# Convolution opening prepared in the projection's last tiles, and the mixer's first steps prepared in the chunk pass

## What is computed

```python
def implicit_filters(L, w1, b1, freq, w2, b2, w3):
    ...
    hdn = jnp.sin(f32(freq[0]) * (feats @ f32(w1) + f32(b1)))
    hdn = jnp.sin(f32(freq[1]) * (hdn @ f32(w2) + f32(b2)))
    filt = (hdn @ f32(w3)).reshape(L, HYENA_ORDER, D_HYENA)
    ...
    filt = filt * jnp.exp(-offset[:, None, None] * rates)
    return filt * lax.rsqrt(jnp.sum(filt * filt, axis=0, keepdims=True) + RMS_EPS)

def hyena_mixer(u_hy, zh, rows, conv_w, conv_b, filt, fbias):
    ...
    z = x1 * fft_long_conv(v, filt[:, 0], fb[0])
    y = x2 * fft_long_conv(z, filt[:, 1], fb[1])
    return y * jax.nn.silu(zh.astype(jnp.float32))
```

## Time and profile before

| | us |
|---|---|
| median of 3 runs | 1657.27 (1656.33 to 1658.02) |
| the profiled execution | 1656.43 |
| its span, first to last instruction | 1654.7 |
| PE busy | 1577.1 |
| DVE, ACT, POOL busy | 711.5, 672.9, 307.3 |
| mean granted clock of PE | 0.984 of full speed |

### The profile page before, as it was taken

How to read it: one execution, slowest core, us unless ns; L and a number is a source line. 1 busy time by engine, 2 the same in 40 slices (tenths; PEclk the granted TensorE clock), 3 DMA queues, 4 the chain that set the end, 5 groups by cost and what they waited for, 6 DMA issues and landing times. The chain is left out here.

```text
span 1654.7 us, 23549 instructions
## 1 busy us (share of the span) xinstructions
PE 1577.1 (95%) x8886; PEld 1357.0 (82%) x8886; DVE 711.5 (43%) x1123; ACT 672.9 (41%) x1371; POOL 307.3 (19%) x297
## 2 busy tenths in 40 slices
PE   8799999999999999999999599999999787999997
PEld 3688888888888888888887599989898776888886
DVE  1754420333333333010100686777675566555553
ACT  2885212333222222131211455555555375545551
POOL 1552000000000000000000031311212125666661
PEclk9899999999999999999999799999999999999999
DMA  9231621222222122121111563647445475566651
GB/s 362 83 116 59 217 70 49 80 76 76 70 76 76 70 76 95 51 98 49 45 51 49 226 154 91 186 103 203 91 116 151 170 216 160 180 208 201 195 179 52
DMA packets 128192, 201.72 MB, mean 122 GB/s; under 512 B 12556, under 2 KB 75714, under 8 KB 121191
## 3 DMA queue, kind: packets, MB, share of 16 engines
q1 hardware_dynamic: 128102, 200.52, 38.3%
HBM read 122.45 MB, written 52.86 MB: 106 GB/s over the span
## 5 line engine op out<-in xcount | busy, mean ns | idle before, releaser
L454 PE MATMUL bank<-h_hi,w_hi 128*128 128x512 f32 (+1 forms) x840 | 324.8, 387 | 0.0
L456 PE MATMUL bank<-h_hi,w_lo 128*128 128x512 f32 (+1 forms) x840 | 322.9, 384 | 0.0
L455 PE MATMUL bank<-h_lo,w_hi 128*128 128x512 f32 (+1 forms) x840 | 322.9, 384 | 0.0
L455 PEld LDWEIGHTS bank<-h_lo,w_hi 128*128 128x128 f32 x840 | 158.3, 188 | 31.2 <-issue 0.2
L456 PEld LDWEIGHTS bank<-h_hi,w_lo 128*128 128x128 f32 x840 | 158.2, 188 | 31.3
L454 PEld LDWEIGHTS bank<-h_hi,w_hi 128*128 128x128 f32 x840 | 158.3, 188 | 30.8 <-issue 0.2
L822 DVE SCALAR_TENSOR_TENSOR work<-work,coef 128x504 f32<-128x504 f32 (+1 forms) x84 | 62.3, 742 | 239.8 <-ACT work L610 239.7
L454 PE MATMUL bank<-w_hi,h_hi 128*128 128x512 f32 (+1 forms) x448 | 164.5, 367 | 0.0
L455 PE MATMUL bank<-w_lo,h_hi 128*128 128x512 f32 (+1 forms) x448 | 164.1, 366 | 0.0
L456 PE MATMUL bank<-w_hi,h_lo 128*128 128x512 f32 (+1 forms) x448 | 164.1, 366 | 0.0
L600 ACT ACTIVATE work<-bank 128x512 f32<-128x512 f32 (+1 forms) x72 | 40.4, 562 | 299.2 <-PE bank L456 299.2
(11 more groups left out here) (228 smaller groups left out, 2841.2 us busy)
## 6 DMA issues: line engine op xcount, KB each, us to landing
H<-spectrum SPq DMA_DIRECT2D x192, 128.0 KB, 2.4
stage<-in_w_in SPq DMA_DIRECT2D x18, 1024.0 KB, 5.6
s_hy<-work SPq DMA_DIRECT2D x48, 256.0 KB, 2.2
xin<-s_hy SPq DMA_DIRECT2D x8, 1024.0 KB, 5.1
kq<-s_k SPq DMA_DIRECT2D x32, 256.0 KB, 4.4
v<-s_v SPq DMA_DIRECT2D x32, 256.0 KB, 5.1
mb<-s_rows SPq DMA_DIRECT2D x32, 256.0 KB, 5.7
late<-in_x SPq DMA_DIRECT2D x16, 512.0 KB, 4.9
```

The source lines that it names most:

```text
L454: pe.matmul(out, lhs[0], rhs[0], start=(k == 0), stop=False)
L455: pe.matmul(out, lhs[0], rhs[1], start=False, stop=False)
L456: return pe.matmul(out, lhs[1], rhs[0], start=False, stop=(k == KD - 1))
```

## The change

**In the projection's last tiles.** SP loads `w3`, the window and the bias behind the second `zh` tile and the first signal tile `xin` behind the ninth. ACT copies `hidden` to the high halves of `layer` and rounds `w3` after its tenth tile; DVE makes the low parts behind its last work there. For that, a memory map common to the three blocks (`Opening`, `Early`) puts these tiles at fixed places above `hidden`, and one `ident` serves all blocks.

**In the opening of `hyena`.** SP issues `outer`, the tables and `back` first, then `w3` and the window of group 1, then `xin`, the spectrum, and only then the gates `x2` and `zh`. ACT loads the table for the root first and squares `f` in four parts; PE sums these 16 pieces itself, in 16 matmuls with `ones`. The signal's outer stage stands ahead of the filter's; its rows and turns stand behind the filter's inner stage.

**In the chunk pass.** The loads for steps 0 and 1 stand one burst behind every second chunk from 5 on. ACT makes `weights(0)` in chunks 14 and 15 and `inter(0)` in chunks 16 and 17; POOL scales `q` of step 0 and step 1 and covers step 1 ahead of its loop. Step 1's scaled `q` has a buffer of its own (half of `z`). `out_hyena(0)` stands in step 1, behind its scores; DVE's `low_hyena(0)` behind the products of step 0.

The diff, cut to what the prediction speaks of (in the order: SP, ACT and DVE of `project`; SP, POOL, PE, ACT and DVE of `mixer`; the tile list, SP, PE, ACT and DVE of `hyena`):

```diff
+                if m == 1:
+                    sp.wait_ge(w_lo_ready, 19)
+                    sp.wait_ge(gate_out, 16)
+                    opening.load_third(sp, d, 0)
+                    opening.load_bias(sp, d, 0)
+                if m == 8:
+                    for slot in range(4):
+                        sp.wait_ge(stored[slot], 16 * len(range(slot, O0, 4)))
+                    sp.wait_ge(tile_ready, Z0 + B_TILES // 2)
+                    opening.load_x(sp, s, 0)
...
+                if m == 9:
+                    act.wait_ge(hid_ready, 4)
+                    act.wait_ge(w_lo_ready, 19)
+                    for e in range(2):
+                        high = slice(e * HALF_P, (e + 1) * HALF_P)
+                        act.copy(opening.layer[high, e, :], hidden[high, :]).then_inc(opening.layer_hi, 1)
+                    act.wait_ge(opening.group_in, 32)
+                    act.copy(opening.w3_hi[:, :], opening.w3[:, :]).then_inc(opening.w3_high, 1)
...
+            dve.wait_ge(opening.layer_hi, 2)
+            layer, w3_hi = opening.layer, opening.w3_hi
+            for e in range(2):
+                high, low = (slice(h * HALF_P, (h + 1) * HALF_P) for h in (e, 1 - e))
+                dve.tensor_tensor(layer[low, e, :], hidden[high, :], layer[high, e, :].bitcast(F32), ALU.subtract)\
+                   .then_inc(opening.layer_lo, 1)
+            dve.wait_ge(opening.w3_high, 1)
+            dve.tensor_tensor(opening.w3_lo[:, :], opening.w3[:, :], w3_hi[:, :].bitcast(F32), ALU.subtract)\
+               .then_inc(opening.w3_low, 1)
...
-            for c in range(SLOTS, 13):
-                load_kv(c)
...
-            sp.wait_ge(early.y_out, 16 * GROUPS)
-            load_yh(0)
-            load_rows(0)
-            load_kv(13)
-            load_kv(14)
-            load_fin(0)
-            load_kv(15)
-            sp.dma_start(gate[:, :], spread(s["gate"][0])).then_inc(gate_in, 16)
-            load_kv(16)
-            load_rows(1)
-            load_kv(17)
+            for c in range(SLOTS, NT):
+                load_kv(c)
+                if c == 5:
+                    sp.wait_ge(early.y_out, 16 * GROUPS)
+                    load_yh(0)
+                    load_rows(0)
+                if c == 7:
+                    load_rows(1)
+                if c == 9:
+                    load_fin(0)
+                if c == 11:
+                    sp.dma_start(gate[:, :], spread(s["gate"][0])).then_inc(gate_in, 16)
+                if c == 13:
+                    load_yh(1)
+                if c == 15:
+                    load_fin(1)
             load_first_q(1)
             load_first_q(0)
-            load_fin(1)
-            load_yh(1)
...
+            for dr in range(2):
+                scale_q(0, dr)
+            cover(1)
+            for dr in range(2):
+                scale_q(1, dr)
+            for n in range(1, NT_LAT + 2):
+                if 1 < n < NT_LAT:
                     scale_q(n, 0)
                 if 0 < n <= NT_LAT:
                     gates(n - 1)
-                if n < NT_LAT:
+                if 1 < n < NT_LAT:
...
-                if n == 0:
+                if n == 1:
                     out_hyena(0)
...
+                if c in (NT - 4, NT - 3):
+                    weights(0, c - (NT - 4))
+                if c in (NT - 2, NT - 1):
+                    inter(0, c - (NT - 2))
             take_backward(NT - 1)
...
             high_hyena(0)
             for dr in range(2):
-                weights(0, dr)
+                inter(1, dr)
             for n in range(NT_LAT + 2):
-                if n < NT_LAT:
+                if 1 < n < NT_LAT:
...
-            low_hyena(0)
...
+                if n == 0:
+                    low_hyena(0)
...
+    tiles = in_time_tiles("P") + signal_tiles("P", "turn") + [("P", "norm", 0)] + signal_tiles(0, "x_outer")
+    tiles += filter_outer_tiles("P") + [("P", "norm", 1)] + filter_rows_tiles("P") + inner_pairs("P", None)
+    tiles += signal_tiles(0, "x_rows") + signal_tiles(0, "turn")
+    return tiles + unit_body(0, True) + unit_tiles(1, True)
...
-            load_group(0)
-            sp.dma_start(ident[:, :], d["ident"]).then_inc(start_in, 16)
-            load_x(0)
             sp.dma_start(outer[:, :], d["outer"].rearrange("p a k -> p (a k)")).then_inc(start_in, 16)
...
+            sp.wait_ge(w3_low, 1)
+            for t in (W_TILES - 2, W_TILES - 1):
+                wait_taken(sp, 0, ("P", "in_time", t))
+            opening.load_third(sp, d, 1)
             wait_filled(sp, 0, ("P", "turn", F_TILES - 1))
-            load_x(GROUPS)
-            load_gates(0)
+            opening.load_x(sp, s, GROUPS)
...
             spread_spectrum(0, "P")
+            load_gates(0)
...
+                    if not (isinstance(g, int) and g == 0):
+                        opening.load_third(sp, d, g + 1)
+                    opening.load_bias(sp, d, g + 1)
...
-            pe.wait_ge(start_in, 32)
-            pe.wait_ge(x_in, 16)
-            turn_x(0, "P")
-            norm(0, "P", 0, 0)
-            pe.wait_ge(f_ready, 1)
-            for t in range(S_TILES):
-                outer_tile(0, ("P", "f_outer", t), f[:, 0], t)
-            norm(0, "P", 1, 1)
-            filter_rows(0, "P")
...
+            pe.wait_ge(x_in, 16)
+            turn_x(0, "P")
+            pe.wait_ge(const_set, 2)
+            dst = bank[wait_bank(0, ("P", "norm", 0))][:, 0:P]
+            for n in range(N2):
+                if n % 4 == 0:
+                    pe.wait_ge(square_part, n // 4 + 1)
+                mm = pe.matmul(dst, ones[:, :], in_Bf[:, n, :], start=(n == 0), stop=(n == N2 - 1))
+            mm.then_inc(summed, 1)
+            pe.wait_ge(start_in, 16)
+            outer_signal(0, 0)
+            pe.wait_ge(f_ready, 1)
+            for t in range(S_TILES):
+                outer_tile(0, ("P", "f_outer", t), f[:, 0], t)
+            norm(0, "P", 1, 1)
...
+            signal_rows(0, 0)
+            turn_next(0, 0)
...
-                high = slice(e * HALF_P, (e + 1) * HALF_P)
-                act.copy(layer[high, e, :], hidden[high, :]).then_inc(layer_hi, 1)
-            high_w3(0, 1)
             act.wait_ge(const_set, 2)
-            square(0, "P", 0, Bf)
+            act.activation(total[:, 0:1], guard[:, 0:1], ACT.Sqrt)
+            for i in range(4):
+                for t in (2 * i, 2 * i + 1):
+                    wait_taken(act, 0, ("P", "in_time", t))
+                cut = slice(4 * i, 4 * i + 4)
+                act.activation(in_Bf[:, cut], f[:, 0, cut], ACT.Square).then_inc(square_part, 1)
             take_turned(0, "P", nat)
-            square(0, "P", 1, B)
             root(0, "P", 0)
+            square(0, "P", 1, in_A2f)
+            take_outer(0, 0, "x_outer", B, 2)
             take_outer(0, "P", "f_outer", Bf, 1)
             root(0, "P", 1)
             take_filter_rows(0, "P")
             for t in range(Q_TILES):
                 take_spectrum(0, "P", t)
+            take_signal_rows(0, 0)
+            high_w3(0, 2)
+            take_turned(0, 0, x1)
...
-            sum_squares(0, 0, Bf)
             invert(0, "P", 0)
+            take_outer(0, 0, "x_outer", B, (1,))
             scale(0, 0, 0)
-            sum_squares(0, 1, B)
+            take_outer(0, 0, "x_outer", B, (3, 5, 7))
+            sum_squares(0, 1, in_A2f)
             invert(0, "P", 1)
...
+            take_signal_rows(0, 0)
+            take_turned(0, 0, x1)
+            low_w3(0, 2)
```

More of the change, by code:

```diff
@@ L1738, in filter_rows_tiles, with signal_tiles, unit_head, unit_body @@
     return [(u, "f_rows", t) for t in range(Q_TILES)]
[L1741 to L1751 removed]
+def signal_tiles(o, stage):
+    return [(o, stage, t) for t in range({"x_outer": S_TILES, "turn": F_TILES, "x_rows": Q_TILES}[stage])]
+def unit_head(o, more):
+    return signal_tiles(o, "x_outer") + (signal_tiles(o, "turn") if more else []) + signal_tiles(o, "x_rows")
+def unit_body(o, ahead):
+    more, tiles = ahead or o == 0, []
     if more:
@@ L2075, in inverse, with outer_signal @@
                 mm.then_inc(summed, 1)
[L2077 to L2079 removed]
+            def outer_signal(g, o):
                 for t in range(S_TILES):
@@ L2212, in unit @@
                 more = ahead or o == 0
-                take_outer(g, o, "x_outer", B, 2)
-                if more:
-                    take_turned(g, o, nat if o else x1)
-                for t in range(0, Q_TILES, 2):
-                    take(g, (o, "x_rows", t), A2[:, 4 * t:4 * t + 4])
+                if not (isinstance(g, int) and g == 0 and o == 0):
+                    take_outer(g, o, "x_outer", B, 2)
+                    if more:
+                        take_turned(g, o, nat if o else x1)
+                    take_signal_rows(g, o)
                 if more:
                     take_outer(g, o, "f_outer", Bf, 1)
-                    if ahead and o == 0:
+                    if ahead and o == 0 and not (isinstance(g, int) and g == 0):
                         high_w3(g, 2)
```

(10 more changed lines are left out.)

358 lines of the change are left out of this document (188 added, 170 removed).

## The result

The changed kernel took 1627.96 us (median of 4 runs, 1626.60 to 1629.02); the kernel before, beside it, 1657.38 us. The ratio is 0.9825, 95% interval 0.9809 to 0.9841: 29.4 us less, where 26.1 were forecast (1631). Its profiled execution took 1629.02 us with a span of 1627.2, so the trace has to account for 27.5 us (1654.7 - 1627.2).

What follows compares the result with a forecast made beforehand. PE, busy 95% of the span, bounds the kernel; only its 77.6 us not busy or half clock can yield. Opening 14.3, chunk pass 3.8 and first steps 8.0 sum to 26.1 us: from 1657.27 to 1631 us, range 1624 to 1644.

Steps and rivals of the forecast that it cites:

- The opening: Start of the convolution to the signal's first inner tile: PE's waits and half clock shrink, 14.3 us gained.
- The first steps: Mixer, scores of step 0 to numerators of step 1: 23.7 us become 15.7, 8.0 us gained.
- The chunk pass: Mixer's chunk pass: 7.0 us from spread loads, less 2.4 for ACT and 0.8 for bursts, 3.8 us gained.
- With the spreading the 4.13 and the 1.20 go: Chunk pass: spreading loads removes two PE waits for `v` and 1.7 us of half clock, 7.0 us in all.
- 0.8 against it: Chunk pass: cost of all load bursts meeting the loads of chunks 6 to 16, taken as 0.8 us.
- rival 1: Bursts hold up the chunk pass; two late ones cost 11.6 us, giving 1643 us; 20% chance.
- ACT's term of 2.4: Chunk pass, chunks 14 to 17: ACT's table load and exponentials put it behind, costing 2.4 us.
- Rival 2: Opening: PE, moved ahead, waits for ACT and DVE again; half of the 14.3 us, 1638 us; 8% chance.
- rival 3: Convolution's inner tiles: the spectrum `H` arrives 3 us late for DVE, giving 1634 us; 10% chance.
- Rival 4: Before the first inner tile: the clock falls in the run of transposes, 1.6 us, giving 1633 us; 3% chance.

Runs made afterwards that it cites:

- the experiment on `out_hyena(0)`: Changed kernel with out_hyena(0) back between the scores and numerators of step 0, the rest of the mixer as changed: ratio 0.9891 to the kernel before.
- The old order of loads: Changed kernel with SP's mixer loads for steps 0 and 1 back behind chunk 12: 1630.76 us.
- the second profile: The changed kernel run again with no edit, also called repeated: 1633.13 us against 1654.81 for the kernel before.
- opening alone: Changed kernel with the mixer's whole old order put back, keeping the new opening and memory map: 1639.78 us against 1655.80 for the kernel before.

## Right and wrong, step by step

**The opening: right.** 14.3 us were forecast to the first inner tile. The eight profiles with the changed opening give 36.9 to 39.2 against 53.0, that is 13.8 to 16.1. PE idle before it is 3.50 us as worked out, the sixteen matmuls of the norm 3.74 (3.7), from the filter's rows to the inner tile 12.44 (12.4), the scale's chain is hidden by 0.4 us. The half clock that the forecast counted there is in seven of the eight; the first profile is the eighth, and has 1.2 to 2.3 us less. What was counted at nothing, group 1's `w3` made early, is worth most of the 1.0 us of B: PE's wait of 0.75 us for `w_lo` at 975.49 is gone.

**The first steps: right.** 8.0 us forecast; E fell by 7.5 in the first profile and by 7.6 when repeated. The first wait was taken at 1.4 us and is 1.91. DVE made it by 0.76 us, where 0.7 was worked out, and the experiment on `out_hyena(0)` shows the mechanism: without it PE waits for these products again.

**The chunk pass: wrong in its terms.** The sum was 3.8 us; D fell by 1.4 in the first profile and by 3.4 in the second. The step that failed is "With the spreading the 4.13 and the 1.20 go ... 7.0 in all", with 0.8 against it. The old order of loads is within 0.3 us of the new one, and with it the waits that spreading was to remove are 2.7 to 3.4 us, with no half clock behind them, not 7.0. The wait for a load did not go, it moved to chunk 6, whose `k` and `v` stand behind the first burst and take 6 us: 2.3 us and 1.7 of half clock (5 us at 0.66). The prediction named this mechanism (rival 1, "a wait of PE for `v` at chunk 6") and priced one such burst at 5.8; it is 4.0, and it happens once, not twice. ACT's term of 2.4 was probably too high (1.2 to 1.5 by one profile). That the sum of 3.8 comes near the 3.4 of the second profile is luck: too much on the gain's side, too little for the bursts. What of D's 1.4 to 3.4 us belongs to the change stays open: "opening alone", with the old mixer, has 54.9, of which 2.1 us are a late `v` of chunk 4 and 1.7 half clock behind it.

**The sum.** Against the repeated profile the span fell by 23.4 us: A 13.8, B 1.0, D 3.4, E 7.6, less 2.8 of half clock in C, with 0.4 for the ends. The first fell by 27.5: A 16.1, B 1.0, D 1.4, E 7.5, and 1.5 for the ends. The forecast of 26.1 lies between them, and 1628 and 1633 are both in its range. That it comes so near is in part luck, since the 2.8 of C and most of the difference between the two profiles are falls of the clock that the forecast did not have as a term.

**The other rivals.** Rival 2 falls: no wait of the old opening came back. So does rival 3: the first product runs at 945.76, 0.2 us behind its tile, and the spread of `H` from 936.41 on held up none. Rival 4 falls: from 940.0 to 944.5, through row transposes and turns alone, the granted clock was 1.00. So it was from 956.9 to 961.0 in the kernel before, the part of that stretch that holds nothing else; the window from 955, which the prediction shows for it, still has 1.8 us of the signal's outer stage. The Trainium skill ("TensorE: Matmul & The Clock Gate", Part 4: PE-mode transpose) would have it fall; the measurement decides.

## What to carry to other kernels

An order that puts independent work of the bottleneck's engine under a chain of the others gave more here than making the chain shorter: the signal's outer stage moved gave 6 us, the sum moved to PE 1.5 and the clock. A wait of two or more microseconds on PE cost its own length and often half clock behind it. Of the eleven waits of 2.0 to 2.8 us in the chunk passes of all profiles but that of the kernel before, seven had half clock within 2 us of their end (3.4 us of it, that is 1.7 us lost, once 6.9 us), and four had none. So price a wait with both, and say that the second part differs between executions. To spread loads over a pass did not help, since each still stands ahead of a load that is needed within the lead; look for which transfer is issued next behind each burst.

## What was not expected of the hardware

The clock falls in other places in other executions of the same instructions. Behind the same 3.50 us of idle time before the opening it was 1.00 through 911 to 916 in one profile and 0.50 in another, and in three it fell about a microsecond after PE had begun at full clock. At the end of the convolution, where PE waits 0.97 us for GpSimd again and again, the fall came early, where PE's waits hid it, or not at all in seven profiles of the changed kernel and its variants (C 342.4 to 342.6), and late in five, where it cost 2.8 us (the thirteenth has 343.1). Each profile has such falls. They can account for the 7 us between the runs of the repeated kernel: the mean granted clock is 0.993 in the fastest (1627.70) and 0.987 in the slowest (1634.72), a difference of 0.6%, or 10 us of full clock (0.006 x 1630). Only one of these runs has a trace, so where they fell in the others is not shown.

Matmuls without use went with a clock that stayed. In both kernels that had 3.1 us of them in front of the first barrier, it was 2.4 GHz through the opening, where it fell in seven of eight without. At the second barrier it is clearer: in all twelve profiles without them a stretch of half clock begins between 0.5 us before and 2 us after the mixer's first transpose, in neither of the two with them.

The 256 KB load of chunk 4's `v` landed in 3.1 to 3.9 us in twelve profiles and took 5.2 and 5.6 in two, with no burst ahead of it. Chunk 6's, behind a burst of 768 KB, took 5.1 to 7.4.
